# Squares of q and k summed by two reduced-precision products of their high and low part, with the chunk preparation started later

## The reference

```python
def l2_normalize(x):
    return x * lax.rsqrt(jnp.sum(x * x, axis=-1, keepdims=True) + EPS)
...
    q = l2_normalize(q.reshape(bsz, s, GDN_HEADS, GDN_DK))     # 8 heads of 128
    k = l2_normalize(k.reshape(bsz, s, GDN_HEADS, GDN_DK))
...
    a_mat = jnp.einsum('bchid,bchjd->bchij', kb, k) * decay * strict
    t_mat = a_mat + jnp.eye(CHUNK, dtype=jnp.float32)
    ...
    sol = lax.linalg.triangular_solve(t_mat, rhs, left_side=True, lower=True, unit_diagonal=True)
```

## Time and profile before

| what | value |
|---|---|
| median of 3 runs | 2468.01 us |
| profiled execution: time of its own | 2469.87 us |
| profiled execution: span of the trace | 2468.1 us, 29891 instructions |
| TensorE busy | 2384.2 us, 97% of the span |
| VectorE busy | 1708.3 us, 69% |
| ScalarE busy | 888.4 us, 36% |
| GpSimd busy | 1368.6 us, 55% |
| TensorE clock granted over the whole | 0.989 of full |

### The profile page before, as it was taken

One profiled execution on the slowest core, in us unless ns is written; L12 is line 12 of the kernel. 1 busy time (PEld: TensorE's weight loads), 2 busy tenths in 40 slices (PEclk: granted clock), 3 DMA queues, 4 the chain that ended last, 5 costly groups with the idle time before them and its releaser, 6 DMA issues. The chain is left out here.

```text
span 2468.1 us, 29891 instructions
## 1 busy us (share of the span) xinstructions
PE 2384.2 (97%) x11396; PEld 1964.4 (80%) x11396; DVE 1708.3 (69%) x1535; ACT 888.4 (36%) x1065; POOL 1368.6 (55%) x747
## 2 busy tenths in 40 slices
PE   7999999899999999989999899999999999999998
PEld 6888888677778888878878678888888888878776
DVE  4987999335774656743334887677676788999986
ACT  5234443545513233431014544334333333433332
POOL 2336887545544454533363265565565557897663
PEclk9999999999999999999999999999999999999999
DMA  6232334687674757554242222222222342232432
GB/s 225 88 94 89 116 103 152 200 283 267 219 244 151 229 173 234 185 172 170 75 146 84 87 71 84 85 85 68 102 76 76 103 162 77 102 119 87 139 114 96
DMA packets 260123, 335.35 MB, mean 136 GB/s; under 512 B 44766, under 2 KB 205867, under 8 KB 253867
## 3 DMA queue, kind: packets, MB, share of 16 engines
q1 hardware_dynamic: 181786, 279.81, 33.4%
q10 hardware_dynamic: 78224, 54.01, 6.9%
HBM read 230.50 MB, written 103.28 MB: 135 GB/s over the span
## 5 line engine op out<-in xcount | busy, mean ns | idle before, releaser
L495 POOL TENSOR_SCALAR w_hi<-w_raw 128x1024 fp32r<-128x1024 f32 x99 | 118.7, 1199 | 552.0 <-issue 478.9
L510 PE MATMUL ps<-act_hi,w_hi 128*128 128x512 f32 x944 | 383.4, 406 | 7.0 <-ACT ring_b L1231 2.5
L514 PE MATMUL ps<-act_hi,w_lo 128*128 128x512 f32 x944 | 368.6, 390 | 0.0
L513 PE MATMUL ps<-act_lo,w_hi 128*128 128x512 f32 x944 | 368.1, 390 | 0.0
L497 POOL TENSOR_TENSOR w_lo<-w_raw,w_hi 128x1024 fp32r<-128x1024 f32 x99 | 273.9, 2767 | 8.3
L2173 POOL TENSOR_TENSOR w_lo<-sm,w_hi 128x512 fp32r<-128x512 f32 x120 | 209.0, 1743 | 116.4 <-ACT w_hi L2578 116.4
L2173 POOL TENSOR_TENSOR w_lo<-w_raw,w_hi 128x512 fp32r<-128x512 f32 x90 | 138.9, 1545 | 152.4 <-ACT w_hi L2578 152.4
L510 PEld LDWEIGHTS ps<-act_hi,w_hi 128*128 128x128 f32 x944 | 177.7, 188 | 47.7 <-issue 6.2
L513 PEld LDWEIGHTS ps<-act_lo,w_hi 128*128 128x128 f32 x944 | 177.8, 188 | 38.1 <-issue 4.1
L514 PEld LDWEIGHTS ps<-act_hi,w_lo 128*128 128x128 f32 x944 | 177.3, 188 | 37.8
L2311 PE MATMUL ps<-t,w_hi 128*128 128x512 f32 x480 | 187.1, 390 | 0.2 <-POOL w_lo L2173 0.2
(11 more groups left out here) (421 smaller groups left out, 5871.7 us busy)
## 6 DMA issues: line engine op xcount, KB each, us to landing
w_raw<-in_w_in_dram SPq DMA_DIRECT2D x34, 1024.0 KB, 6.4
kept_c<-ring_a ACTq DMA_DIRECT2D x36, 512.0 KB, 3.2
w_raw<-in_w_ffn_down_dram SPq DMA_DIRECT2D x18, 1024.0 KB, 5.0
w_raw<-in_w_ffn_up_dram SPq DMA_DIRECT2D x16, 1024.0 KB, 5.2
w_raw<-in_w_ffn_gate_dram SPq DMA_DIRECT2D x16, 1024.0 KB, 5.2
f_cm<-ring SPq DMA_DIRECT2D x32, 512.0 KB, 2.6
dn_raw<-f_cm SPq DMA_DIRECT2D x24, 512.0 KB, 4.4
qkv_a<-kept_c SPq DMA_DIRECT2D x7, 1536.0 KB, 6.8
```

The lines of the kernel that those rows point to most:

```text
L495: nc.gpsimd.tensor_scalar(hi, raw, 1.0, 0.0, ALU.mult, ALU.add).then_inc(split_done, 1)
L510: first = nc.tensor.matmul(o, wh, mov[0][:, k, c], start=(k == 0), stop=False)
L513: nc.tensor.matmul(o, wh, mov[1][:, k, c], start=False, stop=False)
L514: last = nc.tensor.matmul(o, wl, mov[0][:, k, c], start=False, stop=(k == KD - 1))
```

## The change

1. **Sums.** ScalarE, after it has squared k and q of a chunk, makes a float32r copy of the squares (`sq_hi`); VectorE subtracts it from the squares and gets the low part (`sq_lo`, new function `squares_low`). TensorE multiplies both by ones in float32r and accumulates: 8 matmuls of 128x512 (4 for the high, 4 for the low part). `ones` gets the type float32r, with a float32 view for its other uses. `sums` waits for the low part (`a_kd`, now counted 3 per chunk) instead of for the square.
2. **Order on VectorE.** The low part of chunk c+1 is made at the end of chunk c, after L1592 and ahead of the substitution's share; that of chunk 0 ahead of everything else.
3. **Starts.** The chunks start at other steps; the last chunk's gram comes at step 128, behind all steps, and its `k_rows` behind the first plain gate tile, which moves into `pe_a`. On ScalarE the first tile is taken out ahead of the first squares.
4. **Substitution** in shares of 18, 20 and 25 operations.
5. **Mixer.** `d_store` of the second half comes after the first `copy_r`. The last gate tile's 8 steps, which stood behind the last chunk, are spread within it, and tile 11 is taken out earlier in that chunk.

```diff
-    ones = sb("ones", [P, P])
+    ones_r = sb("ones", [P, P], f32r)
+    ones = ones_r[:, :].bitcast(f32)
...
         def main(c, more):
-            steps = (2, 2, 2, 2, 2, 1, 1) if c < 4 else (2, 1, 1, 1, 1, 1, 1)
+            steps = (2, 2, 2, 2, 2, 1, 1) if c < 4 else (2, 1, 1, 1, 1, 1, 1) if c < NCH - 1 else (3, 2, 2, 1, 3, 2, 3)
...
             main(c, c < NCH - 1)
-        gemm(KD)
...
             if more:
                 copy_r(c + 1)
-            if c in (0, 2):
-                mg_evict({0: 2, 2: 5}[c])
+            if c in (0, 2, 7):
+                mg_evict({0: 2, 2: 5, 7: 11}[c])
...
             act.dma_start(y_c[:, 0:KD, tokens(c)], yssm[:, :, :]).then_inc(ys_kept, 16)
-            if c == 7:
-                mg_evict(11)
...
         mg_evict(0)
-        d_store(act, 1)
         ready_to_mix(act)
         copy_r(0)
+        d_store(act, 1)
...
-    A_START = [14, 28, 41, 55, 70, 85, 100, 116]
+    A_START = [20, 33, 45, 57, 71, 86, 101, 116]
     A_AT = [(s, s + 4, s + 9, s + 12) for s in A_START]
+    A_AT[NCH - 1] = (116, 120, 128, 129)
...
-                after(pe, a_sq, 2 * c + i + 1)
+                after(pe, a_kd, 3 * c + i + 1)
                 if i == 0:
                     after(pe, a_gd, 4 * c)
-                else:
-                    after(pe, a_kd, c)
                 for half in range(2):
-                    last = t.matmul(bank(2 * i + half), ones[:, :], flat(sqn_a[:, at + 4 * half:at + 4 * half + 4, :]),
-                                    start=True, stop=True)
+                    heads = slice(at + 4 * half, at + 4 * half + 4)
+                    t.matmul(bank(2 * i + half), ones_r[:, :], flat(sq_hi[:, heads, :]), start=True, stop=False)
+                    last = t.matmul(bank(2 * i + half), ones_r[:, :], flat(sq_lo[:, heads, :]), start=False, stop=True)
...
+        pe_unit(pe, U_MG, O_MG, 0, mov=mov)
+        k_rows(NCH - 1)
...
                 a(sqn_a[:, at:at + 8, :], qkv_a[:, at:at + 8, :], ACT.Square).then_inc(a_sq, 1)
+            for i, at in enumerate((8, 0)):
+                after(act, a_sq, 4 * c + i + 1)
+                a(sq_hi[:, at:at + 8, :], sqn_a[:, at:at + 8, :], ACT.Copy).then_inc(a_sq, 1)
...
+        evict(0)
+        past(act, c_prod, PRODUCTS * C_PAIRS)
+        past(act, c_evicted, SUMMED * C_PAIRS)
         squares(0)
-        evict(0)
         evict(1)
...
+        def squares_low(c):
+            for i, at in enumerate((8, 0)):
+                after(dve, a_sq, 4 * c + i + 3)
+                sq = sqn_a[:, at:at + 8, :]
+                v.tensor_tensor(sq_lo[:, at:at + 8, :], sq, sq_hi[:, at:at + 8, :].bitcast(f32), ALU.subtract).then_inc(a_kd, 1)
+
+        squares_low(0)
...
             v.tensor_tensor(bk_a[:, 1], hd(bank(2, 2)), wide(col(c, WD_A), P), ALU.mult).then_inc(a_kd, 1)
+            if c < NCH - 1:
+                squares_low(c + 1)
             if 4 <= c < 7:
-                substitute(dve, 0, (0, 26, 52, SUB_STEPS)[c - 4:c - 2])
+                substitute(dve, 0, (0, 18, 38, SUB_STEPS)[c - 4:c - 2])
...
-            after(sp, a_kd, c + 1)
+            after(sp, a_kd, 3 * c + 3)
...
         pe_a(pe)
-        pe_unit(pe, U_MG, O_MG, 0, mov=mov)
         a_ended(pe)
```

More of the change, by code:

```diff
@@ L206, in hybrid_block_kernel @@
     sub_d = sb("sub_d", [P, 1024], f32, sub)
+    fill_sq = sb("fill_sq", [P, 27], f32, sub)
+    sq_hi = sb("sq_hi", [P, 16, P], f32r, sub)
+    sq_lo = sb("sq_lo", [P, 16, P], f32r, sub)
     sub.close()
@@ L1697, in a_ended @@
     def a_ended(eng):
-        for s, per in ((a_rs, 4), (a_bv, 1), (a_gd, 4), (a_kd, 1)):
+        for s, per in ((a_rs, 4), (a_bv, 1), (a_gd, 4), (a_kd, 3)):
             after(eng, s, NCH * per)
```

## The result

The changed kernel takes 2474.09 us, median of 12 runs (2468.79 to 2480.95), where the kernel before takes 2468.35 (12 runs): ratio 1.0023, 95% interval 1.0014 to 1.0032. It is slower by 5.7 us; 13.3 us faster was forecast. The profiled execution took 2470.15 us (span 2468.3), the profiled one of before 2469.87 (2468.1). So the two traces differ by 0.3 us and the medians by 5.7. The other 5.4 us lie between executions, and what the records give for each is its mean granted clock: 0.989 in both profiled executions, 0.985 to 0.989 over the 12 of the changed kernel, mostly 0.986 to 0.988. Three executions that lie far outside the others (6212 us of the kernel before, 13526 us in e4, 3417 us in e9) are left out of every ratio.

A forecast was written before the change was run, and what follows sets the result against it. TensorE's own work, busy 97% of the span, was taken as the bound. Terms 13.0 + 4.4 - 4.7 + 4.5 - 1.6 - 0.3 - 2.0 = 13.3 us off 2468.01 gave 2454.7 us, range 2443 to 2463.

The forecast's parts named there:

- Step 1: Sums on TensorE: eight reduced products take 1.81 us instead of 3.44 in each of 8 chunks, saving 13.0 us.
- Step 2: Start of stage A: TensorE's first stall shrinks and the v_rows wait goes, saving 4.4 us.
- Step 3: Hand-over between chunks: longer chain of load, squares, copy and low parts stalls TensorE in three hand-overs, costing 4.7 us.
- The slower rival: Hand-over sets stage A's pace: 30.3 us of cost, 2480 us, decided past 2.6 us mean stall per hand-over; chance 8%.
- Step 4: Substitution's new shares: gram 5 on time, gram 6 still late and slow, gram 7 without stall; saves 4.5 us.
- Step 5: End of stage A: 1.6 us lost behind chunk 7's k_rows, then a late second substitution costs 0.3 us net.
- Step 6: Mixer's last chunk: waits filled, but a 6 us hole opens at the tail's first unit; costs 2 us.
- The sum: Whole kernel: all terms together save 13.3 us, giving 2454.7 us.
- The sign that the prediction itself named: Stage A: forecast is wrong if the sums' waits exceed 10 us in all, or if the gram waits vanish altogether.
- the length of a stall: TensorE's clock: a stall of 1.85 us or more is priced 1.7 to 2.6 us above its length.

The follow-up runs named there:

- e4: Changed kernel without computing low parts, the high part multiplied twice instead: 2449.46 us, ratio 0.9914 to the kernel before.
- e9: Changed kernel with VectorE's low parts of the next chunk ahead of the scaling of k: 2469.98 us, ratio 1.0009 to the kernel before.
- e5: Changed kernel with ScalarE making square and high part per half, k first, straight from q and k: 2473.50 us, ratio 1.0022.
- e7: e5 with q, k and v loaded in three transfers, each issued when its part of the buffer is free: 2473.93 us, ratio 1.0018.
- e10: e9 on top of e7, low parts first and load in three: 2454.40 us, ratio 0.9946 to the kernel before.
- e6: Changed kernel with GpSimd's 32 decay passes cut from 128x1024 to 128x8 elements: 2450.88 us, ratio 0.9927 to the kernel before.
- e12: Changed kernel with chunk starts 14 steps apart (the last two gaps 13): 2468.81 us, ratio 0.9995 to the kernel before.
- e14: e9 with the high parts of e5, load in one transfer: 2465.69 us, ratio 0.9983 to the kernel before.
- e11: e2 (old sums) with GpSimd's 32 decay passes cut as in e6: 2445.68 us, ratio 0.9910 to the kernel before.
- e2: Changed kernel with the old full-precision sums, no copy or low part: 2452.09 us, ratio 0.9934 to the kernel before.
- e17: e10 with the starts of e12 and the substitution in four shares: 2448.68 us, ratio 0.9921 to the kernel before.
- e3: Kernel before with only the mixer's new last chunk: 2470.09 us, ratio 1.0000 to the kernel before.
- e8: e2 with the mixer's old last chunk: 2451.07 us, ratio 0.9927 to the kernel before.
- e1: Kernel before with only the new sums (high and low parts), everything else as before: 2491.06 us, ratio 1.0088.

## Why the prediction was wrong

**Step 1, the sums: right.** Undisturbed they take 1.96 us, 0.15 more than forecast, and 3.44 before: 12 us for eight. In the changed kernel only part of that came: from the starts of its products the eight sums take 2.1, 3.0, 3.4, 3.9, 2.0, 2.0, 2.6 and 2.1 us without their waits, 21.1 in all where eight times 1.96 are 15.7, since those of chunks 1, 2, 3 and 6 ran in part at half speed behind their waits.

**Step 2, the beginning: right.** 3.3 us of idleness forecast, 3.3 measured; the wait of `v_rows` gone.

**Step 3, the hand-over: the step that failed.** The place was named; the size was not, and one link of the chain was left out. Forecast were 4.7 us in chunks 1, 3 and 6; measured are 13.2 in nine waits, in all chunks but 4, and 5.4 us of slow clock in the sums themselves, with more in the steps behind them. Together they are more than the products save. Three causes:
- *The order in VectorE's program.* The prediction added load, squares, copies and low parts, and took the sum for the moment at which the low part is ready. It left out the instruction ahead of the low parts on their engine, the scaling of k, which waits for TensorE's `k_rows`. With starts 12 steps apart `k_rows` stands directly ahead of the next sums, so the low part can't be in time, whatever the load does: e5 and e7 nothing, e9 4 us, e10 19. This is what chunks 1 to 3 suffer from: their 9.6 us of waits stay nearly whole without the decay passes (9.0 in e6) and fall to 1.95 with starts 14 steps apart (e12).
- *The load*, as forecast 11 to 12 us of chain, is the second limit right behind: 32.4 us of VectorE's idleness once the order is mended (e9), and some 9 of the 15 us that e10 gains over e9 (e14; the rest are earlier high parts).
- *GpSimd's passes.* They hold the low parts (up to 3.43 us instead of 1.21) and, what the prediction did not carry through, the q product that releases the next load. Cutting those over the decays gives 23 us with low parts and 6 without (e6, e11); the splits of weights, which hold the low parts of chunk 1, were in every run, so their share is not measured. The Trainium skill ("SBUF — State Buffer", section "Who interferes with whom") has the rule that a VectorE instruction with two SBUF inputs contends with a GpSimd instruction that reads SBUF, under an exclusive lock. The trace agrees (4.67 us for two low parts beside a pass of 3.21, 2.35 between passes). The prediction weighed this against each low part alone and not against the whole chain.

The slower rival had the place and two of the causes, the load and the passes, but not the order either, and it asked for 30.3 us. The hand-over's mean price, (13.2 - 0.5 + 5.4) / 7 = 2.6 us without chunk 0's wait, is the one from which it was to decide. Its count of held low parts was the right worry; the prediction's row for it is read a little short (the held operation ended at 624.31 + 2.43 = 626.74, 0.3 us behind the pass, not with it), which changes nothing.

**Step 4, the substitution: half right.** Without the new sums all late gram goes (e2), the upper bound of 11.6 us. With them it went from 7.5 us of waiting to 6.8, in chunks 5, 6 and 7, where gram 5 and 7 were forecast on time. The low parts ahead of each share push it towards the next chunk, and the cheaper sums bring TensorE to the gram sooner (5.3 us of such waits in e4, without low parts); what each does is not separated. That these waits hang on the shares e17 shows (8.8 to 1.2 us).

**Step 5, the end of stage A: right for the first wait** (1.8 for 1.6 us), wrong for the second: 1.6 us on `xinv` for 4.3. So the mixer's start, forecast at -0.3 us, gave 4.1 between the traces. That was luck, and it hid 4.4 us of the loss in stage A.

**Step 6, the mixer's end: right in place and size.** 7.2 us of waiting for `act_lo` for 6; the traces put the whole mixer at -2.9 us (from -1.0 to +2.0) for -2, within the 1.8 us by which they part without a cause, e3 and e8 at 0 and about -1, with intervals of 2 to 3 us to each side.

**The sum.** What was forecast for all but the sums (5.0 us without the hand-over) came out as 16 in e2. By the waits that its trace has no longer: 4.4 for the beginning, 11.6 for the gram and 4.0 for the mixer's start, where no wait came in place of `rinv`, less 1.8 and 2.9 at the two ends, 15.3. What was forecast for the sums and their hand-over, +8.3, came out at -22. The first error, a lucky one, hid a part of the second. The sign that the prediction itself named was there: the sums' waits add up to more than 10 us.

Left open: the 5.4 us between the profiled execution and the median. The clock's mean over the executions goes with it; which waits are longer in the slower executions no trace here shows.

## What to carry to other kernels

When a product is made cheaper by an operation on another engine, write down that engine's program around the new operation: its earliest start is the end of what stands ahead of it, which may wait for the very engine that is to be relieved. Where two limits lie close behind one another, mending either alone shows little (0 and 4 us here, 19 together), and a null result doesn't clear the suspect. Split a change in two, too, before believing it: here its other half was worth 16 us, and hid behind a loss of 22.

## What the runs showed that was not expected

Waits cost more than their length, by the clock: its mean over the span was 0.991 to 0.992 in the executions of e2 and 0.983 to 0.986 in those of e1. Of 2470 us, 0.007 is 17 us, so up to 17 of the 39 that lie between the two. But the length of a stall does not tell whether the clock falls, as the prediction had it (1.85 us or more): behind 2.12 us gram 5 kept its time (3.72), where before it took 5.41 behind 1.85, and in e10 5.41 behind 2.14. And in chunk 1's sums the same 1.95 us was followed by products 0.43 us apart in the changed kernel, where a wait of 1.40 had come just ahead, and by products 0.24 apart in e12, where it stood alone. What decides between the two no run here shows.

GpSimd is held as well as VectorE: in the changed kernel the subtraction of the decays took 2.88 us beside chunk 0's q product, which ended at 467.89, where its shortest takes 1.89:
```profile
466.77 2.88 POOL L1637 TENSOR_TENSOR dec_a<-dec_a,tmc 128x1024 f32<-128x1024 f32 x1
```
So an operation put on one of the two engines is paid for on the other as well.
